# Opening the expert layers of a two-block network: all dot products of head 0 and the search of head 2 ahead of the norms of tiles 1 to 3

## The reference, cut to what matters

```python
# SEQ = 512 tokens, D_MODEL = 1024, 16384 experts, 8 heads, 16 experts per head and token
x = x + g1 * (y @ w_out)                                  # first block; the second: h + y @ w_o
h = modulate(rmsnorm(x, norm2_w), sh2, sc2)               # second: rms_norm(h, g_ffn)
q = (h @ w_q).reshape(tokens, 8, 2, 128)                  # per head two halves
s1, s2 = q[:, :, 0] @ k1.T, q[:, :, 1] @ k2.T             # 128 scores each
v1, i1 = top_k(s1, 16); v2, i2 = top_k(s2, 16)
cand = v1[..., :, None] + v2[..., None, :]                # 256 sums
top_s, pos = top_k(cand, 16); idx = i1 * 128 + i2 at pos
g = softmax(top_s)
act = gelu(einsum("thkd,td->thk", down[idx], h))          # 16 dot products of 1024 per head
x = x + g2 * einsum("thk,thkd->td", g * act, up[idx])     # 16 weighted rows per head
```

## Time and profile before

| | |
|---|---|
| median of 3 runs | 4043.13 us (4020.12 to 4047.68) |
| the profiled execution | 4008.87 us |
| its span, first to last instruction | 4007.2 us |
| outside the span | 1.67 us |
| expert layer 1, first to last up gather | 574 to 2193 us |
| expert layer 2, likewise | 2329 to 3962 us |

### The profile page before, as it was taken

How to read it: one execution, slowest core, us unless ns; L and a number is a source line. 1 busy time by engine, 2 the same in 40 slices (tenths; PEclk the granted TensorE clock), 3 DMA queues, 4 the chain that set the end, 5 groups by cost and what they waited for, 6 DMA issues and landing times.

```text
span 4007.2 us, 30795 instructions
## 1 busy us (share of the span) xinstructions
PE 1871.4 (47%) x10149; PEld 1003.8 (25%) x10149; DVE 2006.4 (50%) x4999; ACT 674.2 (17%) x1905; POOL 2070.1 (52%) x2099
## 2 busy tenths in 40 slices
PE   8997974232222333342378953232223332222485
PEld 3554541111111211121033631111111211111131
DVE  1324266556565555666411465565655555565210
ACT  2112121111111111111121121111111111111221
POOL 1412236555555555665665155555555555565663
PEclk9999786666666666666689976666666666666697
DMA  5312358888888878998999578888888777898995
GB/s 202 126 53 84 124 191 340 309 315 321 310 328 306 313 294 308 369 392 321 385 332 362 202 282 306 313 324 317 324 313 305 294 305 307 346 362 330 339 366 229
DMA packets 338224, 1167.08 MB, mean 291 GB/s; under 512 B 37114, under 2 KB 40468, under 8 KB 336916
## 3 DMA queue, kind: packets, MB, share of 16 engines
q0 software_dynamic: 294912, 1073.87, 70.2%
q1 hardware_dynamic: 43156, 91.26, 6.3%
HBM read 1162.90 MB, written 2.10 MB: 291 GB/s over the span
## 4 chain that ended last, share of the span: by engine, by line
another core or an unknown queue 34%; PE 24%; issue 14%; DVE 7%; DMA 6%; ACT 5%; POOL 5%; SPq 0%; DVEq 0%; ACTq 0%; POOLq 0%
PE banks L784 18%; PE banks L1131 5%; POOL ring L735 3%; DMA ring<-in_expert_v,idx_v 2%; ACT ring L1529 2%; DVE scr L2091 2%; DMA scr<-in_peer_down,idx 1%; DMA ring<-in_peer_up,idx_v 1%; POOL scr L723 1%; DMA scr<-in_expert_u,idx 1%; ACT L1516 1%; ACT L1511 1%; PE banks L1099 0%; ACT scr L1511 0%
## 5 line engine op out<-in xcount | busy, mean ns | idle before, releaser
L2091 DVE CUSTOM_DVE_ANT_0 scr<-scr,banks 128x1024 f32<-128x1024 f32 x1024 | 1219.5, 1218 | 644.8 <-DMA scr<-in_expert_u,idx 258.7
L1131 PE MATMUL banks<-ring 128*32 128x512 f32 x3712 | 606.5, 772 | 630.5 <-DMA ring<-in_peer_up,idx_v 245.5
L735 POOL DMA_INDIRECT ring<-in_expert_v,idx_v x464 | 440.9, 950 | 503.6 <-PE banks L1131 355.6
L735 POOL DMA_INDIRECT ring<-in_peer_up,idx_v x464 | 443.5, 956 | 477.1 <-PE banks L1131 305.3
L1099 PE MATMUL banks<-ring,const 128*32 128x16 f32 x1024 | 38.2, 214 | 1362.8 <-ACT ring L1521 862.2
L723 POOL DMA_INDIRECT scr<-in_expert_u,idx x512 | 480.7, 939 | 273.1 <-issue 139.7
L723 POOL DMA_INDIRECT scr<-in_peer_down,idx x512 | 482.9, 943 | 226.9 <-issue 137.5
L1099 PEld LDWEIGHTS banks<-ring,const 128*32 128x32 f32 x1024 | 39.4, 148 | 1443.4 <-issue 1419.0
L784 PE MATMUL banks<-ring,scr 128*128 128x128 f32 (+1 forms) x2112 | 390.9, 366 | 8.1 <-ACT ring L1507 4.6
L784 PEld LDWEIGHTS banks<-ring,scr 128*128 128x128 f32 x2112 | 363.6, 269 | 27.2 <-issue 22.9
L1131 PEld LDWEIGHTS banks<-ring 128*32 128x32 f32 x3712 | 124.1, 129 | 947.8 <-issue 919.8
(11 more groups left out here) (232 smaller groups left out, 2246.4 us busy)
## 6 DMA issues: line engine op xcount, KB each, us to landing
ring<-in_w_mod SPq DMA_DIRECT2D x12, 2048.0 KB, 8.5
ring<-in_w_in SPq DMA_DIRECT2D x7, 2048.0 KB, 12.9
scr<-in_peer_w_q SPq DMA_DIRECT2D x1, 8192.0 KB, 28.0
scr<-in_peer_down,idx POOLq DMA_INDIRECT x512
scr<-in_w_q SPq DMA_DIRECT2D x4, 2048.0 KB, 8.3
scr<-in_expert_u,idx POOLq DMA_INDIRECT x512
ring<-in_peer_up,idx_v POOLq DMA_INDIRECT x464
ring<-in_expert_v,idx_v POOLq DMA_INDIRECT x464
```

The source lines that it names most:

```text
L735: nc.gpsimd.indirect_dma_start(up_rows[slot], None, table_v, bass.IndirectOffsetOnAxis(idx_v[:, n % V_HEADS, col_of(k):col_of(k) + 1], 0)) ...
L1131: last = nc.tensor.matmul(psum[2 + c][32 * g:32 * g + 32, :], spread[:, n % 2, k, :], up_rows[slot + g][:, c * CW:(c + 1) * CW], start=(h ...
L2091: V.tensor_tensor_reduce(u_rows[:, k % SLOTS, :], u_rows[:, k % SLOTS, :], xn, 1.0, 0.0, ALU.mult, ALU.add, dots[:, n % 2, k:k + 1]).then_ ...
```

## The change

In both openings the same steps are put into another order; no arithmetic is added or left out.

- DVE: after the first eight dot products of head 0 comes tile 1's projection (in layer 1 its second half), then at once the other eight. The norm scales of tile 1 come after them, then the softmax and indices of head 1, tile 2's projection, `weights(0)`, the search of head 2, four dot products of head 1, the indices of head 2, tile 3's projection. The scales of tiles 2 and 3 stand between and behind the dot products of head 1.
- PE: the three projections and the scores of head 2 follow each other; the turned rows (`tile_rows`) of tiles 1, 2 and 3 are hung behind batches 0, 2 and 4. `move_idx(1)` goes ahead of `scores(2)`.
- ACT: only tile 1 is squared in the opening. `gelu_of(0)`, `weights_out(0)` and `spread_out(0)` come ahead of the squares of tiles 2 and 3, and the `tile_out` of tiles 1, 2, 3 are hung behind batches 0, 2 and 4.
- PSUM: the projections of tiles 1, 2, 3 use banks 6/7, 2/3, 6/7 (before: tile 1 banks as they came or 2/3, tiles 2 and 3 both 2/3), and all turned rows use 6 and 7.

```diff
@@ plan_jobs, layer 1 (layer 2 likewise) @@
-    jobs.add(("wo", 1, 1), "D", 6)
-    for t in (2, 3):
+    jobs.add(("wo", 1, 1), "D", 7)
+    for t, bank in ((2, 2), (3, 6)):
         for n in range(2):
-            jobs.add(("wo", t, n), "D", 2 + n)
-    for t in (1, 2):
+            jobs.add(("wo", t, n), "D", bank + n)
+    for t in (1, 2, 3):
         tile("n1", t, (6, 7), "AA")
-    tile("n1", 3, (2, 3), "AA")
@@ PE, start_first (start_second likewise) @@
                 project("wo", 2, w)
+                move_idx(1)
                 scores(2)
                 project("wo", 3, w)
-                tile_rows("n1", 1)
-                tile_rows("n1", 2)
-                move_idx(1)
-                tile_rows("n1", 3)
-                all_empty(pe, "nt", "n1", 3, 1)
+                for half in range(2):
+                    empty(pe, "wo", 2, half)
@@ PE, beside (layer 2 with "gf") @@
+            beside = {0: lambda: tile_rows("n1", 1), 2: lambda: tile_rows("n1", 2), 4: lambda: tile_rows("n1", 3),
@@ ACT, peer @@
                 start(rows_of, scores_out, softmax_exp)
-                activations(0)
+                gelu_of(0)
+                weights_out(0)
                 spread_out(0)
+                softmax_exp(2)
+                for t in (2, 3):
+                    added(projection, t)
+                    tile_square(rows, t)
+                    tile_root(rows, t)
@@ ACT, start_first (start_second: tile 1 ahead of scores_out(2)) @@
                 scores_out(2)
-                for t in (1, 2, 3):
-                    added("wo", t)
-                    tile_square("n1", t)
-                    tile_root("n1", t)
-                for t in (1, 2, 3):
-                    tile_out("n1", t, gains, shifts)
+                added("wo", 1)
+                tile_square("n1", 1)
+                tile_root("n1", 1)
@@ ACT, act_after (layer 2 with "gf") @@
+            act_after = {0: lambda: tile_out("n1", 1, in_gain, in_shift), 2: lambda: tile_out("n1", 2, in_gain, in_shift),
+                         4: lambda: tile_out("n1", 3, in_gain, in_shift), 93: ...
@@ DVE, peer; the old openings end with pack_idx(0) @@
+                def open_heads():
+                    route(1)
+                    route_keys(1)
+                    dve.wait_ge(xn_ready, n0 // PH + 1)
+                    dot_products(0, range(SLOTS))
+                    add_projection(layer, projection, 1, (1,) if layer == 0 else (0, 1))
+                    dot_products(0, range(SLOTS, TOPK))
+                    tile_stats(rows, 1)
+                    softmax(1)
+                    pack_idx(1)
+                    add_projection(layer, projection, 2)
+                    weights(0)
+                    route(2)
+                    dot_products(1, range(QUADS))
+                    route_keys(2)
+                    add_projection(layer, projection, 3)
+                    dot_products(1, range(QUADS, SLOTS))
+                    tile_stats(rows, 2)
+                    softmax(2)
+                    dot_products(1, range(SLOTS, TOPK))
+                    tile_stats(rows, 3)
+                    pack_idx(2)
...
-                for j in range(1, N_HEADS):
+                for j in range(2, N_HEADS):
                     head(j)
```

More of the change, by code:

```diff
@@ L327, in plan_jobs @@
     jobs.add(("kT", 1, 3), "A", 6)
-    for n in range(2):
-        jobs.add(("wo2", 1, n), "D", 2 + n)
-    for t in (2, 3):
+    for t, bank in ((1, 6), (2, 2), (3, 6)):
         for n in range(2):
-            jobs.add(("wo2", t, n), "D", 2 + n)
-    for t in (1, 2):
+            jobs.add(("wo2", t, n), "D", bank + n)
+    for t in (1, 2, 3):
         tile("gf", t, (6, 7), "AA")
-    tile("gf", 3, (2, 3), "AA")
     def gates(t):
@@ L1280, in start_second @@
                 project("wo2", 2, w)
+                move_idx(1)
                 scores(2)
                 project("wo2", 3, w)
[L1283 to L1287, removed]
+                for half in range(2):
+                    empty(pe, "wo2", 2, half)
             def p_cols(k):
@@ L1500, in _, with peer @@
                 copy_out(yT[:, k, :], "yT", k).then_inc(emptied["A"], 1)
-            def peer(layer, gelu_func, start, beside):
+            def peer(layer, projection, rows, gelu_func, start, beside):
                 n0 = layer * N_HEADS
@@ L1580, in start_first @@
                     copy_out(kT[:, 4 * g:4 * g + 4, :], "kT", 0, g).then_inc(emptied["A"], 1)
-                tile_out("n1", 0, gains, shifts)
+                tile_out("n1", 0, in_gain, in_shift)
                 empty(act, "nt", "n1", 0, 0)
@@ L1630, in _ @@
                     act_after[mixing_batch(15) + 2 + j] = lambda j=j: pool_rows(j)
-            peer(0, ACT.Gelu, start_first, act_after)
+            peer(0, "wo", "n1", ACT.Gelu, start_first, act_after)
             pool_rows(3)
             def start_second(rows_of, scores_out, softmax_exp):
-                gains = lambda k: col("g_ffn_2", k)
                 mid_squares("nf", (3,), (x_added, 1 + TT))
@@ L1645, in start_second @@
                     copy_out(kT[:, 4 * g:4 * g + 4, :], "kT", 1, g).then_inc(emptied["A"], 1)
-                tile_out("gf", 0, gains, no_shift)
+                tile_out("gf", 0, ffn_gain, no_shift)
                 copy_out(u_late[:, :, 16:16 + P], "puL").then_inc(emptied["A"], 1)
@@ L1661, in start_second @@
                 softmax_exp(1)
+                added("wo2", 1)
+                tile_square("gf", 1)
+                tile_root("gf", 1)
                 scores_out(2)
-                for t in (1, 2, 3):
-                    added("wo2", t)
-                    tile_square("gf", t)
-                    tile_root("gf", t)
-                for t in (1, 2, 3):
-                    tile_out("gf", t, gains, no_shift)
             ple_gain = lambda k: col("g_ple_2", k)
@@ L1987, in add_projection, with peer @@
                     V.tensor_tensor(x, o[:, :], x, ALU.add).then_inc(emptied["D"], 1)
-            def peer(layer, start):
+            def peer(layer, projection, rows, start):
                 n0 = layer * N_HEADS
@@ L2125, in head @@
                         pack_idx(j + 1)
-                start(route, route_keys, softmax, dot_products, pack_idx)
-                for j in range(1, N_HEADS):
+                def open_heads():
[20 more added lines that the diff above has]
+                    pack_idx(2)
+                start(route, route_keys, softmax, pack_idx)
+                open_heads()
+                for j in range(2, N_HEADS):
                     head(j)
@@ L2182, in mid_stats @@
                     tile_rstd(name, t)
-            peer(0, start_first)
+            peer(0, "wo", "n1", start_first)
             mid_final((0, 1))
```

47 lines of the change are left out of this document (12 added, 35 removed).

## The result

The changed kernel takes 4010.03 us (median of 21 executions, 3984.22 to 4033.60), the kernel before 4034.08 us in the same comparison (21 executions, 4012.93 to 4063.37). The ratio is 0.9943, 95% interval 0.9921 to 0.9966: 23 us less, between 14 and 32. The forecast was 19 us less, 4024 us from a median of 4043.13. A ratio, here and in the experiments, leaves out executions more than 1.5% above the fastest of the same kernel; where a kernel scatters more widely than that, the median is the fairer reading, and both are given. The profiled execution of the change took 4024.29 us (span 4022.7), 15 us more than that of before. Single executions of either kernel lie up to 1.3% apart here, so the two traces are compared stretch by stretch and not by their ends.

What follows compares the result with a forecast made beforehand. Bound by a loop of 48.4 us per head, where POOL's gathers wait for PE sums that come when transfers drain. Layer 1's 6 us plus layer 2's 13 make 19: 4043.13 - 19 = 4024 us, range 3997 to 4050.

Steps and rivals of the forecast that it cites:

- layer 1 and layer 2 gains of 10 and 16 us: POOL's up gathers at batch 5: start at 641.5 instead of 651.68, and 2388.5 instead of 2404.24.
- forecast of 6 and 13: Net gains of the two layers after give-backs: layer 1 6 us, layer 2 13 us.
- DVE's order: Both openings: head 0's products end at 558.4 (12 us earlier) and 2297.9; layer 2's wait of 21.52 us goes.
- PE's last projection and the first up gather: Openings: last projection starts at 553.2 and 2303.3; layer 1's first up gather comes 5 to 7 us earlier than 574.32.
- What is given back: After the first sums (20 and 26 us earlier), later waits leave 17 and 20 us at batch 3, 10 and 16 at batch 5.
- This loop has its own period; a layer that starts x earlier ends x earlier: Middle of the layers: rounds of 48.4 us per head, so an opening's gain passes unchanged to the layer's end.
- The typical round: Middle of a layer: 48.4 us for each head, including POOL's stop of 13.7 us; the change leaves it at 48.
- Rival 1: Turned rows fit idle time of PE and ACT; nearly all kept: 37 us (4006) or 46 us (3997); chance 0.23.
- Rival 2: Openings gain 17 or 20 us, but detours cost twice the estimate: 1 us kept, 4042 us; chance 0.18.
- Rival 3: Turned rows of tiles 2 and 3 wait for drains, breaking POOL's burst: four stops, 55 us, 4061 us; with worse, chance 0.07.
- The rule of the Trainium skill: SBUF engine and DMA ports don't slow each other; turned rows cost only their own time, and rival 1 would result.

Runs made afterwards that it cites:

- e11: The change plus 30 dummy ACT copies ahead of every head's gelu from the third on: 3862.29 us against 4024.70 for the kernel before, ratio 0.9586.
- e12: The kernel before plus 30 dummy ACT copies ahead of every head's gelu from the third on: 3884.20 us against 4025.07 without them, ratio 0.9679.
- e7: The change with ACT's square of tile 1 in layer 2 put back behind head 2's scores: 3988.82 us against 4019.74 for the kernel before, ratio 0.9928.
- e9: The change with every third batch's sum ahead of PE's weight move, index move and first scores: 3913.65 us against 4024.70 for the kernel before, ratio 0.9728.

## Why the prediction was right, step by step

The time was right (19 us forecast; 23 measured, 21.9 in the quieter pair), and the change does shorten both openings. Part of the agreement is luck. At batch 5, where the forecast took its layer 1 and layer 2 gains of 10 and 16 us, the trace has 0.6 and 5.5; three batches later it has 8.0 and 12.8, because in each layer one round happened to last 40 or 41 us. The split of e11 and e12 (6.8 and 11.6 for a forecast of 6 and 13) is that of one execution each, and most of it comes behind the rounds. Several steps that led to 19 were wrong.

- **DVE's order: right.** Head 0's products end at 557.4 and, by layer 2's own beginning, at 2297.9; forecast were 558.4 and 2297.9; the stall of 21.52 us goes. e7 shows that ACT's new place for the square is not needed for the gain.
- **PE's last projection and the first up gather: wrong.** I let the scores of head 2 end at 552.9 as before and put the last projection at 553.2. Freeing the banks did remove the 4.99 us of the earlier trace rows, but the scores' results now wait for the gathers that POOL issues 12 us sooner, and the projection starts at 561.19. In layer 2 the last projection begins at 2311.4 by the layer's own beginning (2334.46 in the trace) for a forecast of 2303.3. The first sums came 14 and 18 us earlier instead of 20 and 26. I had the mechanism at hand and used it in the loop but not here.
- **What is given back: right in kind, too small early.** ACT's root of tile 3 was put at 596 and came at 605.75; head 2's first product was put at 617, and the gather that waits for it stands at 629.11. Batch 3 was kept 10.4 and 13.8 us earlier instead of 17 and 20.
- **"This loop has its own period; a layer that starts x earlier ends x earlier": not shown, and wrong for one execution.** The rows are a long round. Seventeen of the 58 rounds in the trace of before were under 46 us, and I read none of them. The typical round was too long by 2 us (48.4 for a mean of 46.3), and rounds vary by 7 us, so that the profiled pair differs by 30 us in its rounds alone. That 23 and 21.9 us arrive at the end agrees with a gain handed on, but in no pair of traces can it be followed there: in e11 against e12 it is gone by batch 89 of layer 1.
- **Rival 1** (all kept, 4006 or 3997): its condition, that turned rows cost nothing there, is false in the first two rounds. **Rival 2** (nothing kept) is excluded by the interval (14 to 32 us). **Rival 3** (POOL's burst broken by 13.7 us per turned tile): POOL stood 9.05 + 2.60 us in layer 1 and 8.33 + 2.59 us in layer 2 for products of head 2, but that stop stood in place of the next one and not beside it.
- **The rule of the Trainium skill** ("SBUF — State Buffer", "SBUF: two separate sides"), by which PE and ACT never wait on transfers there, is again not what the rows show: 16 us for the scores of head 2 beside gathers, 26 us or 2.0 us for the same weight move. Whether a port is the cause, no row says. By that rule e11 could only lose.

## What to carry to other kernels

When a kernel is bound by a loop of queues, list the length of every round before taking one as typical: if the lengths differ, what moves the program to the shorter ones can be worth several times the edit at hand, here 141 us to 23. An operation whose result others queue behind should be issued when its result can come, not as early as it can: here a delay of some 8 to 10 us in each round was worth over 3% (ratio 0.9679). And a small gain is measured best in the version whose executions scatter least.

## What was not expected of the hardware

- A PE result can take 2 us or 26 us for the same eight small matmuls, depending on whether it is issued in a full burst of gathers (DMA share 1.02 and 416 GB/s from 995 to 998 us in the trace of before) or just behind a pause of POOL (0.85 and 283 GB/s in e11). Larger groups show it as a stutter: some of the sums in e11's opening run as single matmuls 1.4 to 2.1 us apart while gathers are in flight. Why a result waits stays open; no run here tells a port, an instruction queue or a semaphore's path apart.
- Why a late weight move returns at once is shown only as a fact of the timing. That e11 works by this and not by some other shift of ACT's order is supported by ACT's idle time ahead of the copy (1684.7 to 279.1 us) and by e9, in which another order of PE alone, which also makes the move late, gives some two thirds of the gain; it was not isolated further.
- Between versions, the sum of the 58 rounds makes most of the difference of the profiled executions (2686 us before, 2716 after, 2564 in e11, for spans of 4007.2, 4022.7 and 3861.3). That the scatter of one kernel's executions (1.3 to 2.2% for the kernel before, by chip) is made in the same way is likely, and not shown, since each kernel has one trace. It is 0.45% in e11.
